# Mixture-of-experts slots: turned selections and factors through DRAM rows instead of TensorE, and one group of attention heads in the other half of the rows

## What is computed

```python
# attention, per group of heads, causal and windowed
logits = q @ k.T * 64 ** -0.5 + bias          # 64 channels a head
# experts: each token uses the 2 best experts of its best group of 4
h = rms_norm(x, norm_ffn)                      # x * rs * gain
probs = softmax(h @ router_w + router_b)
gates = top_2_of_best_group(probs)             # normalised to sum 1
for e in range(16):
    a = silu(h @ w_gate[e]) * (h @ w_up[e])
    out = out + gates[:, e] * (a @ w_down[e])
```

## Time and profile before

| | us |
|---|---|
| median of 3 runs (588.23 to 588.8) | 588.34 |
| profiled execution: its own time | 590.58 |
| profiled execution: span | 588.8 |
| TensorE busy | 574.5 (98%) |
| VectorE busy | 275.9 (47%) |
| ScalarE busy | 236.1 (40%) |
| transfers: queue of SyncE (q1), 159.44 MB | 70.2% of 16 engines' span |
| transfers: queue of ScalarE (q10), 4.79 MB | 2.3% |

### The profile page before, as it was taken

How to read it: one execution, slowest core, us unless ns; L and a number is a source line. 1 busy time by engine, 2 the same in 40 slices (tenths; PEclk the granted TensorE clock), 3 DMA queues, 4 the chain that set the end, 5 groups by cost and what they waited for, 6 DMA issues and landing times.

```text
span 588.8 us, 7340 instructions
## 1 busy us (share of the span) xinstructions
PE 574.5 (98%) x2896; PEld 385.0 (65%) x2896; DVE 275.9 (47%) x410; ACT 236.1 (40%) x320; POOL 18.2 (3%) x13
## 2 busy tenths in 40 slices
PE   7999999999999999999999999999999999999995
PEld 4888888888876778888888786434444444444333
DVE  4561687876577652998665656211112211110002
ACT  5644763774593644833555532311121121111112
POOL 0000000050010000000100100000000000000000
PEclk8999999999999999999999998999999999999998
DMA  8965484467533328756546893799999999999971
GB/s 309 407 224 205 147 310 151 149 249 243 200 122 109 108 72 299 235 182 214 186 171 200 321 427 164 287 407 426 426 427 426 427 425 426 427 426 425 427 327 73
DMA packets 45932, 164.72 MB, mean 280 GB/s; under 512 B 4164, under 2 KB 5320, under 8 KB 33352
## 3 DMA queue, kind: packets, MB, share of 16 engines
q1 hardware_dynamic: 43840, 159.44, 70.2%
q10 hardware_dynamic: 2056, 4.79, 2.3%
HBM read 163.17 MB, written 1.05 MB: 279 GB/s over the span
## 4 chain that ended last, share of the span: by engine, by line
PE 90%; DVE 3%; ACT 2%; DVEq 1%; DMA 1%; issue 1%; POOL 0%; SPq 0%
PE ps L1902 19%; PE ps L1474 15%; PE ps L1482 15%; PE ps L1475 15%; PE ps L1921 9%; PE ps L1455 5%; PE ps L1946 3%; PE ps L1827 2%; DMA w_raw<-in_w_in 1%; PE ps L1604 1%; PE ps L1630 1%; PE ps L1741 1%; ACT w_hi L524 1%; PE ps L1764 1%; PE ps L1818 1%
## 5 line engine op out<-in xcount | busy, mean ns | idle before, releaser
L906 DVE TENSOR_TENSOR w_lo<-w_raw,w_hi 128x2048 fp32r<-128x2048 f32 (+2 forms) x54 | 118.5, 2211 | 64.3 <-ACT w_hi L524 63.6
L1474 PE MATMUL ps<-w_hi,act_hi 128*128 128x512 f32 (+1 forms) x304 | 119.6, 395 | 2.0 <-ACT w_hi L524 2.0
L1475 PE MATMUL ps<-w_hi,act_lo 128*128 128x512 f32 (+1 forms) x304 | 117.3, 388 | 0.0
L524 ACT ACTIVATE w_hi<-w_raw 128x2048 fp32r<-128x2048 f32 (+2 forms) x54 | 98.9, 1854 | 31.1 <-PE ps L1482 25.2
L1902 PE MATMUL ps<-e_raw,xg 128*64 128x512 f32 x368 | 81.7, 595 | 0.0
L1482 PE MATMUL ps<-w_lo,act_hi 128*128 128x512 f32 (+1 forms) x304 | 74.3, 387 | 0.0
L1474 PEld LDWEIGHTS ps<-w_hi,act_hi 128*128 128x128 f32 x304 | 57.7, 190 | 14.6 <-issue 3.4
L1475 PEld LDWEIGHTS ps<-w_hi,act_lo 128*128 128x128 f32 x304 | 57.8, 190 | 10.8
L1482 PEld LDWEIGHTS ps<-w_lo,act_hi 128*128 128x128 f32 x304 | 55.6, 188 | 11.6 <-issue 0.7
L1902 PEld LDWEIGHTS ps<-e_raw,xg 128*64 128x64 f32 x368 | 25.5, 137 | 49.6 <-issue 49.5
L1394 DVE TENSOR_TENSOR a_st<-e_act,ps 128x256 f32<-128x256 f32 x16 | 6.7, 417 | 95.7 <-ACT e_act L853 95.7
(11 more groups left out here) (286 smaller groups left out, 693.1 us busy)
## 6 DMA issues: line engine op xcount, KB each, us to landing
w_raw<-in_w_in SPq DMA_DIRECT2D x32, 1024.0 KB, 5.3
e_raw<-in_w_expert_down SPq DMA_DIRECT2D x26, 1024.0 KB, 15.7
e_raw<-in_w_expert_gate SPq DMA_DIRECT2D x23, 1024.0 KB, 16.2
e_raw<-in_w_expert_up SPq DMA_DIRECT2D x23, 1024.0 KB, 16.9
w_raw<-in_w_expert_gate SPq DMA_DIRECT2D x9, 1024.0 KB, 12.4
w_raw<-in_w_expert_up SPq DMA_DIRECT2D x9, 1024.0 KB, 14.5
w_raw<-in_w_expert_down SPq DMA_DIRECT2D x6, 1024.0 KB, 15.9
w_raw<-in_w_xkv SPq DMA_DIRECT2D x4, 1024.0 KB, 5.0
```

The source lines that it names most:

```text
L524: A(bview(w_hi, b, blocks[b].shape), bview(w_raw, b, blocks[b].shape), ACT.Copy).then_inc(hi_done, 1)
L906: V.tensor_tensor(bview(w_lo, b, sh), bview(w_raw, b, sh), f32(bview(w_hi, b, sh)), ALU.subtract).then_inc(lo_done, 1)
L1474: MM(o, xh[:, t0 + k, i * P:(i + 1) * P], wh[:, k], start=first and k == 0, stop=False)
L1475: MM(o, xl[:, t0 + k, i * P:(i + 1) * P], wh[:, k], start=False, stop=False)
```

## The change

Experts. `turn_selection`, `selection_out`, and the slot gates of groups 1 to 3 go. Instead one table `by_token` (tokens on partitions; 32 columns of positions, 32 of factor = gate times `rs`, 2 of `rs`) is turned once on TensorE to 66 rows of 128 and written to DRAM (`slot_rows`) by a transfer from ScalarE's queue. Transfers from the same queue read rows back and spread them over the partitions: per group the positions of four experts to all 128 (4 KB each), and for groups 1 to 3 the `rs` row four times to partitions 0 to 63 (`fours`, runs of 1 KB) and the four factor rows to partitions 64 to 127. VectorE compares the spread positions with the partition's slot number (a column `slot`) and has `selT`; it multiplies the factors by it and sums over the tokens, and has `scales`. All scaling is now at gate/up: gate by `rs`, up by `rs` times gate; y is copied without a scale. Selections after group 0 are 64 slots wide instead of 128.

Attention. In the second of the three groups neighbouring heads change places (`swap_neighbours` orders the weights and biases before the launch), so its score product uses the other 64 rows than those of the other two groups, and writes bank 5 while they write bank 4.

Left out of the diff: the constant `slot`, buffers and semaphore names, and the adapted waits of `first_gather`, `gate_up` and `down`.

```diff
-        prob, posm, gates, chosen, topw = (rt(NT * NE) for _ in range(5))
+        prob, chosen, topw = (rt(NT * NE) for _ in range(3))
+        by_token = rt(2 * (2 * NE + 1))
+        by_slot = rt(P)[0:2 * (2 * NE + 1)]
+        posm = by_token[:, 0:NT * NE].rearrange("p (e i) -> p i e", i=NT)
+        factor = by_token[:, NT * NE:2 * NT * NE].rearrange("p (e i) -> p i e", i=NT)
...
         def head_of(u, g):
 
-            return AHG * g + 2 * (u // 4) + u % 2
+            return AHG * g + 2 * (u // 4) + (u + g) % 2
...
+        ROWS = 16 * (1 + 4 + 3 + 3)
+
+        def spread(first, n, parts):
+
+            return bass.AP(tensor=slot_scratch.tensor, offset=first * P, ap=[[0, parts], [1, n * S]])
+
+        fours = bass.AP(tensor=slot_scratch.tensor, offset=4 * NE * P, ap=[[0, SLOTS], [0, EPG], [1, S]])
+
...
-            def selection_out(r, g, half):
-                act.wait_ge(s["sel_turned"], r * (2 * NG) + (2 * g + half + 1))
-                bank = (0 if g else 3) if half else 1
-                A(selT[g % 2][:, 2 * half:2 * half + 2, :], ps[:, bank, :].rearrange("p (e t) -> p e t", e=2),
-                  ACT.Copy).then_inc(s["selT_moved"], 1)
+            def positions_in(g):
+                act.dma_start(f32(selT[g % 2][:].rearrange("p e t -> p (e t)")),
+                              spread(2 * EPG * g, EPG, P)).then_inc(s["rows_spread"], 16)
+
+            def factors_in(g):
+                to = factors[g % 2]
+                act.dma_start(to[0:SLOTS], fours).then_inc(s["rows_spread"], 16)
+                act.dma_start(to[SLOTS:P].rearrange("p e t -> p (e t)"),
+                              spread(2 * NE + 2 * EPG * g, EPG, SLOTS)).then_inc(s["rows_spread"], 16)
...
                 act.wait_ge(mm_done, r * NB2 + used(e, "up", 1))
-                A(gu[:], ps[:, 0, :], ACT.Copy, scale=rs_slot[g % 2][:, j:j + 1]).then_inc(s["gu_moved"], 1)
+                A(gu[:], ps[:, 0, :], ACT.Copy, scale=scales[g % 2][:, j:j + 1]).then_inc(s["gu_moved"], 1)
...
             def y_hi_part(r, e):
-                g, j = e // EPG, e % EPG
-                w_ = w_slot[g % 2][:, j:j + 1]
...
-                    A(y_hi[:], ps[:, 3, :], ACT.Copy, scale=w_).then_inc(s["y_hi_done"], 1)
+                    A(y_hi[:], ps[:, 3, :], ACT.Copy).then_inc(s["y_hi_done"], 1)
...
                     gate_up_out(r, e)
-                    if j == 0:
-                        for half in range(2):
-                            selection_out(r, g, half)
+                    if e == 0:
+                        act.dma_start(slot_scratch, by_slot).then_inc(s["rows_spread"], 16)
+                    if j == 2 and 1 <= g < NG - 1:
+                        positions_in(g + 1)
+                        factors_in(g + 1)
                     gate_silu(r, e)
+                    if e == 0:
+                        act.wait_ge(s["rows_spread"], r * ROWS + 16)
+                        positions_in(0)
+                        positions_in(1)
+                        factors_in(1)
                     if e:
...
-                V.scalar_tensor_tensor(lg[:, 0:2, 0:w], ps[:, 4, :].rearrange("p (g x) -> p g x", g=2)[:, :, 0:w],
-                                       ADH ** -0.5, heads[:, j:j + 5:4, :], ALU.mult, ALU.add)
-                V.scalar_tensor_tensor(lg[:, 2, 0:w], ps[:, 5, 0:w], ADH ** -0.5, heads[:, 8 + j, :], ALU.mult,
-                                       ALU.add).then_inc(s["a_logits_moved"], 1)
+                V.scalar_tensor_tensor(lg[:, 1, 0:w], ps[:, 5, 0:w], ADH ** -0.5, heads[:, head_of(u, 1), :], ALU.mult, ALU.add)
+                V.scalar_tensor_tensor(lg[:, 0:3:2, 0:w], ps[:, 4, :].rearrange("p (g x) -> p g x", g=2)[:, :, 0:w],
+                                       ADH ** -0.5, heads[:, j:j + 9:8, :], ALU.mult, ALU.add).then_inc(s["a_logits_moved"], 1)
...
-            def select_tile(i, g0):
-                return V.tensor_tensor(sel[:, i], bc(iota.unsqueeze(1), (P, EPG, P)),
-                                       bc(v2(posm)[:, i, g0].unsqueeze(2), (P, EPG, P)), ALU.is_equal)
+            def select_tile(i, g):
+
+                n = SLOTS if g else P
+                return V.tensor_tensor(sel[:, i, :, 0:n], bc(iota[:, 0:n].unsqueeze(1), (P, EPG, n)),
+                                       bc(posm[:, i, EPG * g:EPG * g + EPG].unsqueeze(2), (P, EPG, n)), ALU.is_equal)
...
-            def select(r, g):
-
-                dve.wait_ge(s["sel_turned"], r * (2 * NG) + 2 * g)
+            def select(g):
                 for i in range(NT):
-                    ins = select_tile(i, slice(EPG * g, EPG * g + EPG))
+                    ins = select_tile(i, g)
                 ins.then_inc(s["sel_ready"], 1)
 
-            def gates_of(g):
-                for i in range(NT):
-                    ins = V.tensor_copy(gcur[:, i, :, 0:EPG], f32(gates_split[:, i, :, EPG * g:EPG * g + EPG]))
-                ins.then_inc(s["sel_ready"], 1)
-
-            def slot_gates(r, g):
-                dve.wait_ge(s["slot_gates_done"], r * NG + (g + 1))
+            def turned_selection(r, g, issued):
+
+                dve.wait_ge(s["rows_spread"], r * ROWS + issued)
+                V.tensor_scalar(selT[g % 2][:], f32(selT[g % 2][:]), slot, None, ALU.is_equal).then_inc(s["selT_ready"], 1)
+
+            def scales_of(g):
+
+                t_ = factors[g % 2]
+                dve.drain()
+                V.tensor_tensor(t_[:], t_[:], f32(selT[g % 2][:]), ALU.mult)
+                dve.drain()
+                V.reduce_sum(scales[g % 2][:], t_[:], AX.X).then_inc(s["slot_gates_moved"], 1)
+
+            def slot_gates(r):
+                dve.wait_ge(s["slot_gates_done"], r + 1)
 
                 W = 2 * (EPG + 1)
-                every = lambda o, step: ps[:, 1, o:o + (EPG - 1) * step + 1:step]
-                w_, rs_ = w_slot[g % 2], rs_slot[g % 2]
-                V.tensor_copy(w_[:], every(0, W + 1))
-                V.tensor_copy(rs_[:], every(EPG, W))
+                every = lambda half, o, step: ps[half * SLOTS:(half + 1) * SLOTS, 1, o:o + (EPG - 1) * step + 1:step]
+                lower, upper = scales[0][0:SLOTS], scales[0][SLOTS:P]
+                V.tensor_copy(by_slot, ps[0:2 * (2 * NE + 1), 1, P:2 * P])
+                V.tensor_copy(lower, every(0, EPG, W))
+                V.tensor_copy(upper, every(1, 0, W + 1))
                 dve.drain()
-                V.tensor_tensor(w_[:], w_[:], every(EPG + 1, W + 1), ALU.add)
-                V.tensor_tensor(rs_[:], rs_[:], every(W - 1, W), ALU.add).then_inc(s["slot_gates_moved"], 1)
+                V.tensor_tensor(lower, lower, every(0, W - 1, W), ALU.add)
+                V.tensor_tensor(upper, upper, every(1, EPG + 1, W + 1), ALU.add).then_inc(s["slot_gates_moved"], 1)
 
...
-                    V.scalar_tensor_tensor(lo, y, w_slot[g % 2][:, j:j + 1], f32(hi),
-                                           ALU.mult, ALU.subtract).then_inc(s["y_lo_done"], 1)
+                    V.tensor_tensor(lo, y, f32(hi), ALU.subtract).then_inc(s["y_lo_done"], 1)
...
                     if more and j == 0:
-                        gates_of(g + 1)
-                        select(r, g + 1)
-                    if more and j == 1:
-                        slot_gates(r, g + 1)
+                        select(g + 1)
+                    if e == 1:
+                        turned_selection(r, 0, 16 * 5)
+                    if more and j == 3:
+                        turned_selection(r, g + 1, 16 * (5 + 3 * g))
+                        scales_of(g + 1)
...
-            V.tensor_tensor(v2(gates), v2(topw), two(rrec, NE), ALU.mult)
-            dve.drain()
-            V.tensor_copy(gates_split[:, :, 0], v2(gates))
-            dve.drain()
-            V.tensor_tensor(gates_split[:, :, 1], v2(gates), f32(gates_split[:, :, 0]), ALU.subtract)
-            dve.drain()
-            gates_of(0)
+            V.tensor_tensor(rrec, rrec, rs_2, ALU.mult)
+            V.tensor_copy(by_token[:, 2 * NT * NE:], rs_2)
+            dve.drain()
+            V.tensor_tensor(factor, v2(topw), two(rrec, NE), ALU.mult)
+            dve.drain()
+            V.tensor_copy(gcur[:, :, 0, 0:EPG], factor[:, :, 0:EPG])
+            dve.drain()
+            V.tensor_tensor(gcur[:, :, 1, 0:EPG], factor[:, :, 0:EPG], f32(gcur[:, :, 0, 0:EPG]),
+                            ALU.subtract).then_inc(s["sel_ready"], 1)
...
                 for g in range(AG):
-                    hd = AHG * g + 2 * jp + jo
+                    hd = head_of(u, g)
                     r0 = hd % 2 * ADH
-                    ins = MM(ps[:, 4 + g // 2, g % 2 * S:g % 2 * S + w], qkT[r0:r0 + ADH, hd // 2, t * P:(t + 1) * P],
+                    ins = MM(ps[:, 4 + g % 2, g // 2 * S:g // 2 * S + w], qkT[r0:r0 + ADH, hd // 2, t * P:(t + 1) * P],
...
-            def slot_gates(r, g):
-
-                pe.wait_ge(s["sel_ready"], r * (2 * NG) + (2 * g + 2))
-                if g:
```

(46 more changed lines are left out.)

43 lines of the change are left out of this document (21 added, 22 removed).

## The result

The changed kernel took 596.87 us (median of 4 runs, 596.23 to 597.87), the kernel before 588.55 beside it (588.23 to 588.80): a ratio of 1.0143, interval 1.0126 to 1.0161, or 8.3 us slower. 591.9 was forecast (+3.6), with a range of 589.6 to 597. The sign and the mechanism came out as written, the size did not; that the time still fell just inside the range is owed to the room left above the forecast, not to its sum. Most executions of the kernel before lie near 588.5 us and some near 590.5, among them the profiled one; one of 973 us of that kernel, and two of 2582 and 2888 us of the kernel of experiment 1, are left out of the comparisons.

The account below looks back on a forecast made before the run. Expert stage bound by TensorE's queue and nearly equally long full weight transfers. Late block +5.4, filled hole -0.7, attention -1.1 sum to +3.6 us: 588.3 to 591.9 us, range 589.6 to 597.

Parts of the forecast that it names:

- What bounds the kernel: Expert stage: TensorE's queue and full weight transfers nearly equally long; expert 15's second "up" block decides, with 3.2 us margin.
- The price of the transfers, "I take 8.6": Expert stage: 3.67 MB added on ScalarE's queue delay the weight blocks behind them by 8.6 us, at 426 GB/s.
- the "upper" bound of 10.4: Most the added 3.67 MB should cost, in us, at ScalarE's queue average of 2.83 us per MB.
- The check on 325 to 329 us: ScalarE's and SyncE's transfers were taken to run together there at 424 GB/s in sum, so both share one rate.
- The join ("8.6 - 3.2"): Last expert: the "up" block lands 8.6 us late against 3.2 margin, TensorE's saved 5.5 becomes waits, end moves +5.4 us.
- The gain of 0.7 at 382 us: Earlier release after expert 0 and the added loads fill the transfer hole of 270 GB/s at 382 to 384 us: -0.7 us.
- Cover for VectorE ("seven microseconds"): First spread rows land by T + 16, at half the rate beside weights; TensorE needs expert 2's gather copies at T + 23.
- Cover for ScalarE: ScalarE's wait for the write has 10 us of cover before expert 1's gate/up copy; each issue costs up to 2.1 us.
- Attention (-1.1): Scores gain 3.3 us, value products lose 1.1, net -2.2; 1.1 is lost to busy VectorE, leaving -1.1 us.
- "The small packets are dear, or the rows late": Rival: 1 KB factor rows run at half rate, or late spread rows stall TensorE: 594 to 599 us, chance 0.10.
- The falling clock: Rival: TensorE's waits in the last experts bring its clock down, adding 3 to 6 us: 595 to 598, chance 0.06.
- Hidden transfers: Rival: the added transfers stay hidden and TensorE's savings of 5.5 and 1.1 stand: 581.7 us, chance 0.10.

Follow-up runs that it names:

- experiment 1: The kernel before with only the attention part of the change (head order and swapped weights), nothing of the experts: 587.17 us, ratio 0.9969.
- Experiment 7: The kernel of experiment 1 plus seven loads of 128 partitions x 4 KB (3.67 MB) that nothing reads: 591.34 us, ratio 1.0043.
- 11: The kernel of experiment 4 without the loads of positions and factors for groups 2 and 3, 1.57 MB loaded in place of 3.67: 585.96 us, ratio 0.9956.
- experiment 4: The changed kernel with each pair of 64-partition factor loads replaced by one load of 128 partitions x 4 KB, same bytes: 591.09 us, ratio 1.0033.
- Experiment 2: The changed kernel with group 0's comparison and its wait for the rows moved behind expert 2's gather copies and activation: 596.66 us, ratio 1.0131.
- 3: The changed kernel with the rs row written four times, so partitions 0 to 63 read one 4 KB run each: 597.36 us, ratio 1.0138.
- 5: The changed kernel with each pair of factor loads made two loads of 128 partitions x 2 KB: 591.31 us, ratio 1.004.
- 9: The kernel of experiment 1 plus fourteen loads of 64 partitions x 4 KB to partitions 32 to 95 that nothing reads: 591.43 us, ratio 1.005.
- (8): The kernel of Experiment 7 with each of its seven unread loads split into two of 64 partitions x 4 KB: 604.42 us, ratio 1.0267.

## Why the prediction was right and wrong, step by step

- **What bounds the kernel: right.** Experiment 7 adds transfers and nothing else and is 4.2 us slower; 11 takes some away and gets their price back. The block named as deciding is the one on which TensorE waits last.
- **The price of the transfers, "I take 8.6": the step that failed.** The bytes were right, and so was their price where loads go to all 128 partitions (8.4 us in the landing of experiment 7). In the changed kernel it was 14 to 15 us (+14.1 in the landing against 7.9), and the "upper" bound of 10.4, ScalarE's queue average, was too low, for a reason of method: the large transfers in it go to all 128 partitions, while of the added bytes three parts in seven (the pairs of factors) go to a half each. The check on 325 to 329 us was no check at all. ScalarE's two loads are issued there, but hardly any of their data moves there; that queue, in 325 to 329 us of the kernel before (packets, MB, share):

```profile
q10 hardware_dynamic: 27, 0.00, 0.5%
```

  The 424 GB/s were SyncE's alone. So the rows showed a rate for one kind of transfer and I applied it to another. Measured by itself: 5.8 us for three pairs (experiment 4), 1.76 to 1.87 for each further one.
- **The join ("8.6 - 3.2"): right in kind.** 14.1 us later in the landing came out as 10.4 in the stage, a margin of 3.7. Experiment 7's trace has +8.4 and +5.4, a margin of 3.0; by the medians the end moved 4.2. The 3.2 holds to within what the runs tell.
- **The gain of 0.7 at 382 us:** the hole is filled (397 GB/s against 270); what it is worth by itself was not measured.
- **Cover for VectorE ("seven microseconds"): wrong, without a price.** The rows landed 20.5 us after their last issue, not 10, and TensorE stalled for 4.6. Experiment 2 removes this stall and gains nothing. The half loads are only a part of the lateness: in experiment 4 the comparison starts at 391.35 instead of 398.47, still 15.6 us after the last issue. The rest is the forecast's "half the rate": beside the weights these loads get a third of the bytes.
- **Cover for ScalarE: right.** Its issues took 0.6 to 0.9 us each, and it still waits 104.9 us for TensorE.
- **Attention (-1.1): sign right, too small.** 1.8 measured, by the traces and the ratio. The scores gained 0.22 and 0.43 a step, four of each, 2.6 us in place of 3.3; but the value products, priced at 1.1 lost, kept their 0.88 us for 12 records.
- **The rivals.** "The small packets are dear, or the rows late" had the right time, 594 to 599, and both of its mechanisms fall (experiments 2 and 3). The falling clock was there, 0.89 at 555 to 570 us with one set of 16 products at 5.35 us for 3.65, but as a consequence of TensorE's waits, and the block's landing at 572.6, not this set, held the last gate/up products. In the traces of experiments 4, 5, 7 and 9 the mean clock is 0.996 to 0.997, against 0.990 in the changed kernel. Hidden transfers are excluded by 7.
- **Sum.** +10.4 in the stage and -1.8 in the attention make +8.6 for the measured +8.3. Two small slips changed nothing: with 4.79 MB and the added 3.7, ScalarE's queue had to come out at 8.5 MB and not 8.4; and four calls with two more steps of 0.15 are 1.2 us, not 1.1.

Open: why a pair costs 1.8 us, when its 0.52 MB at half the rate would cost 1.2. In (8) of experiments 7 and 8 the rate stayed near 300 for 12 us and moved 3.6 MB, of which only 1.05 MB were the added loads' (29%), so the weights beside them were slowed as well. Not tried: spreading `rs` over all partitions once and only the factors per group; by experiments 4 and 5 I estimate about 591 us for it, still above experiment 1.

## What to carry to other kernels

Before pricing a transfer by the rate of others, compare its shape with theirs: which partitions it goes to and how its source is stepped, not only its bytes; a broadcast to 64 partitions can cost more than one to 128. Where the weights' queue is full to the end, a load that saves a TensorE operation must be cheaper than that operation in transfer time (here 1.2 us for 0.52 MB against 0.8 us saved), or it loses, once the margin of the weights is spent, even when all goes well. A window in which two queues "run together" is a check only if both moved bytes in it: ask for the queues by themselves. A change with two halves is best run as two: one was worth 1.8 us.

## What the runs showed that was not expected

- 64-partition loads to partitions 0 to 63 or 64 to 127 bring the rate of a full queue from 426 to 273 to 303 GB/s while the DMA share column stays at 1.00 or more; to partitions 32 to 95 they do not (430).
- The same 0.52 MB to 128 partitions, from a source whose outermost size is two, took 42 us to land, at the end with a share of 0.12 of the engines.
- Two full queues shared by packets: 232 of 0.86 MB beside 235 of 1.69 MB in 6 us.
- Score products over 64 rows, with the middle group in the other rows (and in the other bank): six records in 0.71 us for 0.93, and in 1.13 for 1.56; value products in column halves that no longer alternate strictly kept their time.
- A load of 4 KB in one run or in four of 1 KB to the same partitions: 597.4 and 596.9 us, no difference.
